# Joint statistics for the two norms around a residual addition, and a first product of four column tiles

## The chip, the cores and the metric

The kernel runs on one NeuronCore of a Trainium2 chip. Its engines are TensorE (PE: matmuls; PEld are its weight loads), VectorE (DVE), ScalarE (ACT), GpSimd (POOL) and SyncE (SP, which here starts the weight DMAs). The metric is the device time of one execution in microseconds, and lower is better. The kernel before takes 2133.98 us (median of three runs, 2133.39 to 2135.55).

## The reference, cut to what matters

The program is a transformer of three blocks over one sequence of 512 positions and 1024 channels. Its first block has a conv layer and an attention layer, and each of them ends in a branch that is normed, gated and added to x, after which x is normed again, scaled and shifted as the input of a gated feed-forward:

```
    for l in range(DEPTH):
        ...
        x = x + g_m * rms_norm(y, norm_g[l, 1])

        h = rms_norm(x, norm_g[l, 2]) * (1.0 + sc_f) + sh_f
        y = conv_ffn(h, ffn_w_in[l], ffn_dw[l], ffn_dwb[l], ffn_w_out[l])
```

Here y is the branch's output (the product with cm_w2 for l = 0, with w_o for l = 1). rms_norm divides each position by the root of its mean square over the 1024 channels. With r the reciprocal root of y's mean square and w = g_m * norm_g[l, 1], the new x is x + w*y*r. The sum of its squares is sum(x²) + 2 r sum(w x y) + r² sum(w² y²): the second norm can be had from three sums that do not need the new x.

## The kernel before, in words

Activations lie transposed: a tile is 128 channels by 512 positions, and there are 8 tiles of x (`XT`), of the normed input h (`Hh`, `Hl`) and of y. Products are done in fp32r with a high and a low part, so a [128 x 128] by [128 x 512] step is three matmuls (`mm3`, lines 291 to 293). Weights come in blocks of 128x1024 from HBM (`fetch`, SP), ACT rounds them to the high part (`split_hi`, line 318) and DVE takes the low part (`split_lo`, line 331). There are three buffers of each part. `split_hi(j)` waits until PE has finished block j-3, `split_lo(j)` follows it, and `fetch(j+3)` waits for `split_lo(j)`.

Each engine's program is written out in order by hand. Generators (`within`, `beside`) interleave side work at each block. In the first feed-forward the side work of DVE is the modulation, a product of 128x1024 (line 629, "mod" below) per step. In the second it is arithmetic on positions (lines 1944 to 1960), which begins with a DMA of the positions that SP starts once the last x tile is written.

A norm goes so: ACT squares the tiles (`square`, line 429), POOL adds six of the eight squares (`gather`, lines 434 and 438), PE sums over the channels with matmuls of a 128x128 slice against a column of ones (`tile_sums`: four matmuls, eight records in the trace, for a tile), DVE makes the mean (`begin_norm`, line 498), POOL the power (`power`, line 518), PE spreads it over the channels (`spread`) into a bank. `fill(n)` issues n matmuls whose result nobody reads.

At the entry of each feed-forward the order is: the norm of y; DVE writes x tile by tile (`add_to_x_dve`, lines 577 and 563), ACT squares it and PE sums (`sums_alone`); a second norm (lines 502, 514, 518, `row_to_cols`); then DVE and ACT make h tile by tile (`make_h_dve`, lines 538 and 543, ACT line 550), while PE multiplies it with the first two column tiles of `ffn_in`. Group by group, two column tiles at a time, each group reads all eight h tiles. After each group ACT takes the two banks (line 1504) and DVE adds two shifted taps (lines 1550 and 1553), which frees the bank; after the second group come the gate and the split of the hidden tile. Five banks rotate: group 0 uses banks 0 and 1, group 1 banks 2 and 3, the next pair of groups 4 and 0, then 1 and 2.

Of the kernel before, what the change touches and what calls it, by code (L numbers as in the profile page):

```python
# [8 lines left out]
F32 = mybir.dt.float32  # L9
# [208 lines left out]
def program(nc, ins, out):  # L218
# [3 lines left out]
    with ctx:  # L222
# [121 lines left out]

        def next_block(hand, name, k0, ahead=AHEAD):
# [77 lines left out]
        ALONE = ("f0", "f1")  # L423
# [17 lines left out]
        def gather_six(s):  # L441
            for t in range(1, 6):
# [10 lines left out]

        def sums_alone(s):
            open_bank(NRM, [(dve_done, ("row", s))])
            fill(11)
            for t in range(DT):
                pe.wait_ge(*act_done["sq", s, t])
                mm(banks[NRM][:, :], ones[:, :], sq[t % 4][:, :], t == 0, t == DT - 1).then_inc(
                    *norm_done.up(("part", s, t), *([("sum", s)] if t == DT - 1 else [])))  # L460
                fill(1 if t < DT - 1 else 3)
# [34 lines left out]
        def begin_norm(s, count, eps=EPS):  # L496
            dve.wait_ge(*norm_done["sum", s])
            dve.e.tensor_scalar(var4, banks[NRM][:, 0:4], 1.0 / count, eps, ALU.mult, ALU.add).then_inc(*dve_done.up(("var", s)))

        def begin_row(s, count):  # L500
            dve.wait_ge(*norm_done["sum", s])
            dve.e.tensor_scalar(part[:, :], banks[NRM][:, :], 1.0 / count, EPS, ALU.mult, ALU.add).then_inc(*dve_done.up(("row", s)))


        def row_to_cols(s):
            open_bank(NRM, [(dve_done, ("var", s))])
            pe.wait_ge(*dve_done["row", s])
            for tb in range(4):
                tok = mm(banks[NRM][:, tb:tb + 1], part[:, tb * P:(tb + 1) * P], ident[:, 0:1], True, True)
            tok.then_inc(*norm_done.up(("cols", s)))  # L510

        def take_cols(s):
            dve.wait_ge(*norm_done["cols", s])
            dve.e.tensor_copy(var4, banks[NRM][:, 0:4]).then_inc(*dve_done.up(("var", s)))
# [80 lines left out]

        def split_ahead(hand):
            presplit(hand, hand.block + AHEAD + 1)
# [2218 lines left out]
```

## Time and profile before

| | us |
|---|---|
| median of 3 runs | 2133.98 |
| the profiled execution | 2137.97 |
| its span in the trace | 2136.2 |
| PE busy in it | 2038.9 (95%) |
| DVE busy | 1294.2 (61%) |
| ACT busy | 853.0 (40%) |
| POOL busy | 169.7 (8%) |

The profiled execution took 3.99 us more than the median, of which 1.8 us lie outside its span. Times in the rows count from the span's start. The first feed-forward's entry runs from about 240 to 318 us, the second's from about 922 to 1005 us.

### The profile page before, as it was taken

The page shows a single profiled execution, that of the slowest core. Times are in us where ns is not written, and L with a number is a line of the kernel's source. Part 1 is how long each engine was busy: PE and PEld are TensorE (multiplying, and loading weights), DVE is VectorE, ACT ScalarE, POOL GpSimd, SP SyncE. Part 2 cuts the span into 40 slices and gives each one's busy share as a digit, 9 for nine tenths or more (in the row PEclk, how much of TensorE's full clock was granted, in tenths as well). Part 3 has the DMA queues.
Part 4 walks back from the last instruction along what each step waited for, and adds up shares of the span by engine and source line. Part 5 has one row for each costly group of instructions (what it writes and reads, how often), then busy time and mean ns, then how long its engine had stood idle before and what let it go on. Part 6 is the DMA issues. An engine that isn't in the chain of part 4 may idle for free.

```text
span 2136.2 us, 26481 instructions
## 1 busy us (share of the span) xinstructions
PE 2038.9 (95%) x10754; PEld 1662.5 (78%) x10756; DVE 1294.2 (61%) x2183; ACT 853.0 (40%) x1430; POOL 169.7 (8%) x112
## 2 busy tenths in 40 slices
PE   5999999999999999899999999999989999999998
PEld 4798778888877976677888887788766788888886
DVE  7666388747836466557765566648876564624632
ACT  3446444324423255534432443332276543412421
POOL 0472100000011000020000000200000010000000
PEclk9999999999999999999999999999999999999999
DMA  8662145655431221112333323222214022332332
GB/s 297 206 209 91 59 148 184 211 195 177 146 110 63 71 68 30 34 46 85 101 107 114 99 93 106 75 78 79 61 49 139 30 90 90 98 99 89 98 99 69
DMA packets 72729, 229.22 MB, mean 107 GB/s; under 512 B 7840, under 2 KB 12832, under 8 KB 72608
## 3 DMA queue, kind: packets, MB, share of 16 engines
q1 hardware_dynamic: 64688, 218.61, 31.7%
q10 hardware_dynamic: 7920, 8.92, 1.2%
q8 instruction: 85, 1.39, 0.3%
q14 instruction: 36, 0.29, 0.0%
HBM read 218.32 MB, written 9.18 MB: 106 GB/s over the span
## 4 chain that ended last, share of the span: by engine, by line
PE 77%; DVE 13%; ACT 5%; issue 3%; POOL 1%; DMA 1%; SPq 0%; DVEq 0%; POOLq 0%; ACTq 0%
PE bank L291 22%; PE bank L293 21%; PE bank L292 21%; PE bank L296 12%; DVE wlo L331 2%; ACT whi L318 1%; PE bank L812 1%; DVE sc L2200 1%; DVE steps L2198 1%; DVE bank L1154 1%; DVE Hl L567 1%; DVE tmp L538 1%; DVE raw L629 1%; DVE Hl L543 1%; DVE XT L563 1%
## 5 line engine op out<-in xcount | busy, mean ns | idle before, releaser
L291 PE MATMUL bank<-Hh,whi 128*128 128x512 f32 x1632 | 653.2, 400 | 22.5 <-DVE wlo L331 9.1
L293 PE MATMUL bank<-Hh,wlo 128*128 128x512 f32 x1632 | 640.7, 393 | 0.0
L292 PE MATMUL bank<-Hl,whi 128*128 128x512 f32 x1632 | 640.5, 392 | 0.0
L331 DVE TENSOR_TENSOR wlo<-stg,whi 128x1024 fp32r<-128x1024 f32 (+1 forms) x299 | 358.5, 1203 | 411.0 <-ACT whi L318 410.5
L318 ACT ACTIVATE whi<-stg 128x1024 fp32r<-128x1024 f32 (+1 forms) x309 | 313.0, 1025 | 395.5 <-PE bank L293 389.2
L291 PEld LDWEIGHTS bank<-Hh,whi 128*128 128x128 f32 x1632 | 309.5, 190 | 94.6 <-DVE wlo L331 12.5
L293 PEld LDWEIGHTS bank<-Hh,wlo 128*128 128x128 f32 x1632 | 309.3, 190 | 65.8
L292 PEld LDWEIGHTS bank<-Hl,whi 128*128 128x128 f32 x1632 | 309.3, 190 | 62.5 <-issue 1.0
L291 PE MATMUL bank<-HIDh,whi 128*128 128x512 f32 x352 | 141.4, 402 | 0.0
L293 PE MATMUL bank<-HIDh,wlo 128*128 128x512 f32 x352 | 137.8, 392 | 0.0
L292 PE MATMUL bank<-HIDl,whi 128*128 128x512 f32 x352 | 137.8, 392 | 0.0
L434 POOL TENSOR_TENSOR part<-sq 128x512 f32<-128x512 f32 x8 | 11.3, 1415 | 1316.3 <-ACT sq L429 1316.3
L291 PE MATMUL bank<-HID2h,whi 128*128 128x512 f32 x256 | 99.7, 389 | 0.0
L293 PE MATMUL bank<-HID2h,wlo 128*128 128x512 f32 x256 | 99.6, 389 | 0.0
L292 PE MATMUL bank<-HID2l,whi 128*128 128x512 f32 x256 | 99.6, 389 | 0.0
L1550 DVE SCALAR_TENSOR_TENSOR tmp<-bank,columns,tmp 128x511 f32<-128x511 f32 x88 | 65.8, 748 | 49.1 <-ACT tmp L1504 49.1
L629 DVE CUSTOM_DVE_ANT_0 raw<-raw,c_act 128x1024 f32<-128x1024 f32 x72 | 87.2, 1219 | 6.6 <-DMA raw<-in_mod_w 6.5
L1504 ACT ACTIVATE tmp<-bank,columns 128x512 f32<-128x512 f32 x88 | 67.8, 770 | 54.7 <-PE bank L293 54.7
L293 PEld LDWEIGHTS bank<-HIDh,wlo 128*128 128x128 f32 x352 | 66.5, 189 | 14.3
L292 PEld LDWEIGHTS bank<-HIDl,whi 128*128 128x128 f32 x352 | 66.5, 189 | 12.7
L291 PEld LDWEIGHTS bank<-HIDh,whi 128*128 128x128 f32 x352 | 66.5, 189 | 12.6
L1513 ACT ACTIVATE HIDh<-tmp 128x512 fp32r<-128x512 f32 x44 | 27.8, 632 | 108.6 <-DVE tmp L1558 108.6
(313 smaller groups left out, 2770.8 us busy)
## 6 DMA issues: line engine op xcount, KB each, us to landing
raw<-in_mod_w SPq DMA_DIRECT2D x96, 512.0 KB, 4.6
stg<-in_ffn_in SPq DMA_DIRECT2D x88, 512.0 KB, 3.9
stg<-in_ff SPq DMA_DIRECT2D x64, 512.0 KB, 3.6
stg<-in_ffn_out SPq DMA_DIRECT2D x40, 512.0 KB, 3.7
stg<-in_cm_w SPq DMA_DIRECT2D x24, 512.0 KB, 4.3
stg<-in_gates SPq DMA_DIRECT2D x16, 512.0 KB, 3.6
stg<-in_z_ch SPq DMA_DIRECT2D x12, 512.0 KB, 3.5
bias_kept<-out_b ACTq DMA_DIRECT2D x20, 256.0 KB, 2.1
```

Of the source, the lines that this page charges most:

```text
L291: pe.e.matmul(out_, l[0], r[0], start=start, stop=False, skip_group_check=True)
L292: pe.e.matmul(out_, l[0], r[1], start=False, stop=False, skip_group_check=True)
L293: return pe.e.matmul(out_, l[1], r[0], start=False, stop=stop, skip_group_check=True)
L296: return pe.e.matmul(out_, l, r, start=start, stop=stop, skip_group_check=True)
L318: act.e.activation(whi[j % NW][:, 0:n * c], stg[j % NSTG][:, 0:n * c], ACT.Copy).then_inc(*w_hi.up(j))
L331: hand.e.tensor_tensor(wlo[j % NW][:, 0:n * c], stg[j % NSTG][:, 0:n * c], whi[j % NW][:, 0:n * c].bitcast(F32), ALU.subtract).then_inc(*m ...
L538: dve.e.scalar_tensor_tensor(tmp[t % 4][:, :], x_tile(t), gain, r[:, :], ALU.mult, ALU.mult).then_inc(*dve_done.up(("hm", ver, t)))
L543: dve.e.scalar_tensor_tensor(Hl[:, t, :], tmp[t % 4][:, :], shift, Hh[:, t, :].bitcast(F32), ALU.add, ALU.subtract).then_inc(*dve_done.up( ...
L629: dve.e.tensor_tensor_reduce(raw[j % NRAW][:, :], raw[j % NRAW][:, :], c_act[:, :], 1.0, 0.0, ALU.mult, ALU.add, modv[:, a:a + 1]).then_in ...
L1504: act.e.activation(at_, bank((("up", l, j), m))[:, :], ACT.Identity, bias=column(bcol + c), scale=column(w3 + 88 + c)).then_inc(*act_done. ...
L1513: act.e.activation(HIDh[:, q, :], at_, ACT.Copy).then_inc(*act_done.up(("hid", l, part, q)))
L1550: dve.e.scalar_tensor_tensor(o[:, 1:S], from_[:, 0:S - 1], column(w3 + 44 + c), o[:, 1:S], ALU.mult, ALU.add).then_inc(*dve_done.up())
```

## The change

The two norms at each feed-forward's entry come from one set of sums. While the branch's last product runs, DVE multiplies y with x and accumulates w·x·y in `tmp[0]` and w²·y² in `tmp[1]` over the first six tiles (conv) or four tiles (attention). PE sums these, and the plain squares, inside the product's last group; the remaining tiles (two or four) are summed each by `joint_tile`, with eight matmuls instead of four. The sum of squares of the old x is kept from the norm before (`keep_var`). A short chain of 128x4 operations on DVE makes the new mean square, POOL raises it, and PE spreads it into bank 5 behind nine fills. Then one loop on DVE makes x and h tile by tile. The first product of the feed-forward works on all four column tiles at once (`gemm_ahead`), the second pair one h tile behind the first. ACT and DVE take its four tiles after all four weight blocks have been passed (`beside_ahead`). The second norm's own squares, sums, row and columns are gone.

The diff, cut to its core:

```diff
         def square(s, t, tile, ready):
             act.wait_ge(*ready)
             if t >= 4:
-                act.wait_ge(*(norm_done["part", s, t - 4] if s in ALONE else pool_done["gathered", s, t - 4]))
+                act.wait_ge(*pool_done["gathered", s, t - 4])
+                if s in GATHERED:
+                    act.wait_ge(*dve_done["acc2", s, t - 4])
...
+        def gather_products(s, Y, g, ready):
+            for t in range(GATHERED[s]):
+                dve.wait_ge(*ready(t))
+                if t > 1:
+                    dve.wait_ge(*dve_done["acc1", s, t - 2])
+                dve.e.tensor_tensor(tmp[2 + t % 2][:, :], Y[t], x_tile(t), ALU.mult).then_inc(*dve_done.up(("xy", s, t)))
+                dve.wait_ge(*act_done["sq", s, t])
...
+                    dve.e.scalar_tensor_tensor(tmp[1][:, :], sq[t % 4][:, :], gain_sq[:, t, 1:2], tmp[1][:, :], ALU.mult,
+                                               ALU.add).then_inc(*dve_done.up(("acc2", s, t)))
...
+                    dve.e.scalar_tensor_tensor(tmp[0][:, :], tmp[2 + t % 2][:, :], g[:, t:t + 1], tmp[0][:, :], ALU.mult,
+                                               ALU.add).then_inc(*dve_done.up(("acc1", s, t)))
+                yield
...
+        def joint_gathered(s):
+            n = GATHERED[s] - 1
+            open_bank(NRM, [(dve_done, ("varx", s))])
+            two_sums(part, pool_done["gathered", s, n], 0, ones[:, 0:1], 1, True, False)
+            two_sums(tmp[1], dve_done["acc2", s, n], 1, ones[:, 0:1], 1, False, False)
+            two_sums(tmp[0], dve_done["acc1", s, n], 8, ones[:, 0:1], 1, False, False)
+
+        def joint_tile(s, t, g):
+            last = t == DT - 1
+            pe.wait_ge(*dve_done["gain_sq", s])
+            two_sums(sq[t % 4], act_done["sq", s, t], 0, gain_sq[:, t, :], 2, False, last)
+            two_sums(tmp[2 + t % 2], dve_done["xy", s, t], 8, g[:, t:t + 1], 1, False, last).then_inc(
+                *norm_done.up(("part", s, t), *([("sum", s)] if last else [])))
+
+        def joint_pe(s, to, g):
+            joint_tile(s, DT - 1, g)
+            fill(3)
+            spread(s, [(dve_done, ("yr", to, DT - 1))])
+            fill(9)
+            spread(to, [(dve_done, ("hm", to, DT - 1))], RX, rx4, pool_done["pow", to])
+            fill(6)
...
+        def joint_dve(s, to, Y, g, gain_, shift_):
+            begin_norm(s, D, at=slice(0, 8, 2))
+            split_ahead(dve)
+            dve.wait_ge(*pool_done["pow", s])
...
+            for t in range(DT):
+                if t > 1:
+                    dve.wait_ge(*dve_done["x", to, t - 2])
+                dve.e.scalar_tensor_tensor(tmp[2 * (t % 2)][:, :], Y[t], g[:, t:t + 1], banks[SPREAD][:, :], ALU.mult,
+                                           ALU.mult).then_inc(*dve_done.up(("yr", to, t)))
+                dve.wait_ge(*dve_done["yr", to, t])
+                dve.e.tensor_tensor(x_tile(t), x_tile(t), tmp[2 * (t % 2)][:, :], ALU.add).then_inc(*dve_done.up(("x", to, t)))
+                if t > 1:
+                    dve.wait_ge(*dve_done["h", to, t - 2])
+                dve.wait_ge(*norm_done["spread", to])
+                dve.wait_ge(*dve_done["x", to, t])
+                dve.e.scalar_tensor_tensor(tmp[2 * (t % 2) + 1][:, :], x_tile(t), gain_[:, t:t + 1], banks[RX][:, :], ALU.mult,
+                                           ALU.mult).then_inc(*dve_done.up(("hm", to, t)))
+                if t == 6:
+                    split_ahead(dve, 1)
+                if t:
+                    low(t - 1)
+            low(DT - 1)
...
+        def gemm_ahead(stage, name, X, by):
...
+            into = [acc_bank((stage, m), by(m)) for m in range(4)]
+            for q in range(DT):
+                product(0, q)
+                if q:
+                    product(1, q - 1)
+            product(1, DT - 1)
+            aside(pe.beside)
+
+        def beside_ahead(hand, name, k0, k1, groups, evac):
+            for _ in range(groups):
+                for i, _ in kparts(k1 - k0):
+                    next_block(hand, name, k0 + i)
+                    aside(hand.beside)
+            for m in range(2 * groups):
+                evac(m)
+            aside(hand.beside)
...
-                    for t in {0: (), 6: (5, 6), 7: (7,)}.get(m, (m - 1,)):
+                    for t in {0: (), 5: (4, 5), 6: (6,), 7: (7,)}.get(m, (m - 1,)):
                         square("cy", t, Y[t], act_done["cy", t])
...
             def tensor():
-                sums_alone(s)
-                row_to_cols(s)
-                fill(4)
-                spread(s, [(dve_done, ("hm", s, DT - 1))])
-                fill(9)
+                gemm_ahead(("up", l, 0), f"ffn_in{l}", HX(s), lambda m: [(dve_done, ("tap2", l, 0, m))])
...
-                beside_gemm(dve, "w_o", 4, DT, 2, evac, 4)
-                gated_gain(gain[1, 1], 1, 2, 1)
-                begin_norm("ay", D)
-                add_to_x_dve("f1", Y, gain[1, 1], [dve_done["gain", 1, 1], norm_done["spread", "ay"]])
+                products = gather_products("ay", Y, gain[1, 1], lambda t: dve_done["ao", t])
+                dve.within[:] = [products]
+                beside_gemm(dve, "w_o", 4, DT, 1)
+                all_of(products)
+                dve.within[:] = []
+                evac_x(4)
+                evac_x(5)
+                beside_gemm(dve, "w_o", 4, DT, 1, evac_x, 6)
+                joint_dve("ay", "f1", Y, gain[1, 1], gain[1, 2], shift(1, 3))
```

How the instructions stand. First PE at the end of the attention layer's last product (tile 6 in bank 0, tile 7 in bank 1; bank 6 takes the sums, `part` the gathered squares, sq2 and sq3 the last two tiles' squares). Before:

```order
L293 MATMUL bank1<-Hh,wlo0 128x512
L296 MATMUL bank6<-ones,part 128x1 x4
L296 MATMUL bank6<-ones,sq2 128x1 x4
L296 MATMUL bank6<-ones,sq3 128x1 x4
L296 MATMUL bank0<-whi1 128x512 x4
L296 MATMUL bank7<-ident,small 128x128 x4
```

After, from the last matmul of tile 7 on:

```order
L293 MATMUL bank1<-Hh,wlo0 128x512
L296 MATMUL bank6<-gain_sq,sq1 128x2 x4
L296 MATMUL bank6<-gains,tmp3 128x1 x4
L296 MATMUL bank6<-gain_sq,sq2 128x2 x4
L296 MATMUL bank6<-gains,tmp2 128x1 x4
L296 MATMUL bank6<-gain_sq,sq3 128x2 x4
L296 MATMUL bank6<-gains,tmp3 128x1 x4
L296 MATMUL bank0<-whi1 128x512 x3
L296 MATMUL bank7<-ident,small 128x128 x4
L296 MATMUL bank0<-whi1 128x512 x9
L296 MATMUL bank5<-ident,small 128x128 x4
L296 MATMUL bank0<-whi1 128x512 x6
```

Ahead of these, inside tile 7, stand 20 more small matmuls: `part`, `tmp1` and `tmp0` between tile 6 and tile 7, and tile 4's eight in the middle of tile 7. The groups of four grew from three to eleven. Second, DVE at the same place: what stands between the low part of the feed-forward's first weight block and the reading of banks 4 and 5 (y's tiles 4 and 5). Before:

```order
L331 TENSOR_TENSOR wlo1<-stg1,whi1 128x1024
L1816 TENSOR_TENSOR Kt<-Kt,bank4 128x512
L1816 TENSOR_TENSOR Kt<-Kt,bank5 128x512
L331 TENSOR_TENSOR wlo2<-stg2,whi2 128x1024
L1816 TENSOR_TENSOR Qt<-Qt,bank0 128x512
```

After:

```order
L524 SCALAR_TENSOR_TENSOR tmp1<-sq2,gain_sq,tmp1 128x512
L531 SCALAR_TENSOR_TENSOR tmp0<-tmp2,gains,tmp0 128x512
L518 TENSOR_TENSOR tmp3<-Kt,XT 128x512
L524 SCALAR_TENSOR_TENSOR tmp1<-sq3,gain_sq,tmp1 128x512
L531 SCALAR_TENSOR_TENSOR tmp0<-tmp3,gains,tmp0 128x512
L1973 TENSOR_TENSOR Kt<-Kt,bank4 128x512
L511 TENSOR_TENSOR tmp2<-Kt,XT 128x512
L1973 TENSOR_TENSOR Kt<-Kt,bank5 128x512
L511 TENSOR_TENSOR tmp3<-Kt,XT 128x512
L331 TENSOR_TENSOR wlo2<-stg2,whi2 128x1024
```

Twelve 128x512 operations, three for each of the tiles 0 to 3, now stand between the split and bank 4; the last five are shown. Third, DVE at the first feed-forward's entry, from the last h tile on. Before:

```order
L543 SCALAR_TENSOR_TENSOR Hl<-tmp3,modv,Hh 128x512
L331 TENSOR_TENSOR wlo2<-stg2,whi2 128x1024
L629 ISA raw0,modv<-raw0,c_act 128x1024
L629 ISA modv 128x1
L331 TENSOR_TENSOR wlo0<-stg0,whi0 128x1024
L1550 SCALAR_TENSOR_TENSOR tmp0<-bank0,columns,tmp0 128x511
L1553 SCALAR_TENSOR_TENSOR tmp0<-bank0,columns,tmp0 128x510
```

After:

```order
L589 SCALAR_TENSOR_TENSOR Hl<-tmp3,modv,Hh 128x512
L732 ISA raw0,modv<-raw0,c_act 128x1024
L732 ISA modv 128x1
L732 ISA raw1,modv<-raw1,c_act 128x1024
L732 ISA modv 128x1
L331 TENSOR_TENSOR wlo1<-stg1,whi1 128x1024
L732 ISA raw2,modv<-raw2,c_act 128x1024
L732 ISA modv 128x1
L331 TENSOR_TENSOR wlo2<-stg2,whi2 128x1024
L732 ISA raw3,modv<-raw3,c_act 128x1024
L732 ISA modv 128x1
L1695 SCALAR_TENSOR_TENSOR tmp0<-bank0,columns,tmp0 128x511
```

Four mods and two splits stand between the last h tile and the taps that free bank 0 (the second of them follows), where one mod and two splits stood. All four tiles' taps follow before the next split.

## Rows read from the trace of the kernel before

**Rows 1.** The page, part 1: busy time and share of the span.

```profile
PE 2038.9 (95%) x10754; PEld 1662.5 (78%) x10756; DVE 1294.2 (61%) x2183; ACT 853.0 (40%) x1430; POOL 169.7 (8%) x112
```

**Rows 2.** Timeline, all engines, conv stage's end: start us, us, engine, line.

```profile
242.27 1.05 PE L296 MATMUL bank<-ones,part 128*128 128x1 f32 x8 [1.67 <-POOL part L438]
...
245.71 1.71 PE L296 MATMUL bank<-ones,sq 128*128 128x1 f32 x8
...
249.73 0.16 DVE L498 TENSOR_SCALAR small<-bank 128x4 f32<-128x4 f32 x1 [10.80 <-PE bank L296]
249.98 1.02 POOL L518 TENSOR_TENSOR small<-small 128x4 f32<-128x4 f32 x1 [7.76 <-DVE small L498]
...
253.44 1.41 DVE L577 SCALAR_TENSOR_TENSOR tmp<-C,gains,bank 128x512 f32<-128x512 f32 x2 [3.54 <-PE bank L296]
...
254.76 0.69 DVE L563 TENSOR_TENSOR XT<-XT,tmp 128x512 f32<-128x512 f32 x1
```

**Rows 3.** Windows: length, busy (x) PE PEld DVE ACT POOL, PEclk, DMA.

```profile
252.00:254.00 2.00, 2.00 (x10) 1.86 (x9) 0.56 (x1) 0.00 (x0) 0.00 (x0) 0.59 0.00 0
...
934.00:936.00 2.00, 2.00 (x17) 1.87 (x16) 0.16 (x1) 0.17 (x1) 0.36 (x1) 1.00 0.07 27
936.00:940.00 4.00, 3.68 (x14) 3.05 (x13) 1.11 (x2) 0.00 (x0) 0.66 (x1) 0.57 0.00 0
```

**Rows 4.** Timeline, DVE and PE, entry of feed-forward 0 and its first column tiles.

```profile
269.11 1.16 PE L296 MATMUL bank<-ident,small 128*128 128x128 f32 x8 [0.32 <-POOL small L518]
...
270.38 1.41 DVE L538 SCALAR_TENSOR_TENSOR tmp<-XT,gains,bank 128x512 f32<-128x512 f32 x2 [2.40 <-PE bank L296]
...
279.85 1.62 DVE L543 SCALAR_TENSOR_TENSOR Hl<-tmp,modv,Hh 128x512 fp32r<-128x512 f32 x2
...
282.81 1.22 DVE L629 CUSTOM_DVE_ANT_0 raw<-raw,c_act 128x1024 f32<-128x1024 f32 x1
...
283.96 1.22 DVE L331 TENSOR_TENSOR wlo<-stg,whi 128x1024 fp32r<-128x1024 f32 x1
...
284.39 0.39 PE L291 MATMUL bank<-Hh,whi 128*128 128x512 f32 x1
...
285.07 0.39 PE L291 MATMUL bank<-Hh,whi 128*128 128x512 f32 x1
...
285.10 0.74 DVE L1550 SCALAR_TENSOR_TENSOR tmp<-bank,columns,tmp 128x511 f32<-128x511 f32 x1
...
287.99 0.75 DVE L1550 SCALAR_TENSOR_TENSOR tmp<-bank,columns,tmp 128x511 f32<-128x511 f32 x1 [1.37 <-ACT tmp L1504]
...
294.60 0.74 DVE L1550 SCALAR_TENSOR_TENSOR tmp<-bank,columns,tmp 128x511 f32<-128x511 f32 x1
...
301.79 1.22 DVE L629 CUSTOM_DVE_ANT_0 raw<-raw,c_act 128x1024 f32<-128x1024 f32 x1
```

**Rows 5.** Timeline, POOL, DVE and PE, attention's end and entry of feed-forward 1.

```profile
923.46 3.53 POOL L438 TENSOR_TENSOR part<-part,sq 128x512 f32<-128x512 f32 x2
...
924.27 1.57 DVE L331 TENSOR_TENSOR wlo<-stg,whi 128x1024 fp32r<-128x1024 f32 x1 [1.65 <-ACT whi L318]
...
932.62 0.95 PE L296 MATMUL bank<-ones,part 128*128 128x1 f32 x8
...
933.43 1.93 PE L296 MATMUL bank<-ones,sq 128*128 128x1 f32 x16
...
935.39 0.16 DVE L498 TENSOR_SCALAR small<-bank 128x4 f32<-128x4 f32 x1 [1.81 <-PE bank L296]
...
955.89 1.41 DVE L538 SCALAR_TENSOR_TENSOR tmp<-XT,gains,bank 128x512 f32<-128x512 f32 x2 [2.47 <-PE bank L296]
...
965.37 1.63 DVE L543 SCALAR_TENSOR_TENSOR Hl<-tmp,modv,Hh 128x512 fp32r<-128x512 f32 x2
...
972.78 0.42 DVE L1944 CAST a<-posi 64x512 f32<-64x512 int32 x1 [4.37 <-DMA posi<-in_pos_q]
...
983.18 0.50 PE L291 MATMUL bank<-Hh,whi 128*128 128x512 f32 x1 [1.49 <-DVE wlo L331]
```

More of the change, by code:

```diff
@@ L343, in presplit, with split_ahead @@
                     fetch(j + NSTG)
+        def split_ahead(hand, more=0):
+            presplit(hand, hand.block + AHEAD + 1 + more)
         def next_block(hand, name, k0, ahead=AHEAD):
@@ L441, in gather_six @@
         def gather_six(s):
-            for t in range(1, 6):
+            for t in range(1, GATHERED.get(s, 6)):
                 gather(s, t)
@@ L494, in fill, with begin_norm @@
                 mm(banks[b][:, :], whi[j % NW][:, 0:P], whi[j % NW][:, 0:S], True, True)
-        def begin_norm(s, count, eps=EPS):
+        def begin_norm(s, count, eps=EPS, at=slice(0, 4)):
             dve.wait_ge(*norm_done["sum", s])
[L498 to L502, printed above, removed]
@@ L505, in row_to_cols @@
[L505 to L514 removed]
+            dve.e.tensor_scalar(var4, banks[NRM][:, at], 1.0 / count, eps, ALU.mult, ALU.add).then_inc(*dve_done.up(("var", s)))
@@ new lines, in weighted, with times_x @@
+        def weighted(s, g):
+            dve.e.memset(gain_sq[:, :, :], 1.0).then_inc(*dve_done.up())
+            dve.wait_ge(*dve_done.now)
+            dve.e.tensor_tensor(gain_sq[:, :, 1], g, g, ALU.mult).then_inc(*dve_done.up(("gain_sq", s)))
+        def times_x(s, t, Y, ready):
+            dve.wait_ge(*ready)
+            if t >= GATHERED[s] + 2:
+                dve.wait_ge(*norm_done["part", s, t - 2])
+            elif t >= GATHERED[s]:
+                dve.wait_ge(*dve_done["acc1", s, GATHERED[s] - 1])
+            dve.e.tensor_tensor(tmp[2 + t % 2][:, :], Y[t], x_tile(t), ALU.mult).then_inc(*dve_done.up(("xy", s, t)))
@@ L516, in power, with joint_act @@
+        def joint_act(to, shift_, used):
+            split_ahead(act)
+            act.wait_ge(*used)
+            for t in range(DT):
+                if t == 5:
+                    split_ahead(act, 1)
+                act.wait_ge(*dve_done["hm", to, t])
+                act.e.activation(Hh[:, t, :], tmp[2 * (t % 2) + 1][:, :], ACT.Identity, bias=shift_[:, t:t + 1]).then_inc(
+                    *act_done.up(("hh", to, t)))
         def power(s):
@@ L701, in gemm_first, with product @@
                             tok.then_inc(*gemm_done.up(*done))
+        def gemm_ahead(stage, name, X, by):
+            blocks = []
+            def product(c, q):
+                while len(blocks) <= 2 * c + q // 4:
+                    blocks.append(next_block(pe, name, 4 * (len(blocks) % 2)))
+                j = blocks[2 * c + q // 4]
+                hi, lo = block_parts(j)
+                xh, xl, ready = X(q)
+                pe.wait_ge(*lo_done(j))
+                pe.wait_ge(*ready)
+                for m in range(2):
+                    o = slice(m * P, (m + 1) * P)
+                    tok = mm3(into[2 * c + m][:, :], (hi[:, q % 4, o], lo[:, q % 4, o]), (xh, xl), q == 0, q == DT - 1)
+                    done = [(stage, 2 * c + m)] if q == DT - 1 else []
+                    if q % 4 == 3 and m == 1:
+                        done.append(("block", j))
+                    if done:
+                        tok.then_inc(*gemm_done.up(*done))
+            into = [acc_bank((stage, m), by(m)) for m in range(4)]
[13 more added lines that the diff above has]
+            aside(hand.beside)
         def beside_first(hand, name):
@@ L1137, in tensor, with gathered @@
                 gemm("w2", "cm_w2", HX("ln"), 0, DT, 1, lambda m: [(act_done, ("cy", m))], 4)
-                pe.within[:] = [sums_within("cy", 6)]
+                def gathered():
+                    for _ in range(6):
+                        yield
+                    joint_gathered("cy")
+                pe.within[:] = [gathered()]
                 gemm("w2", "cm_w2", HX("ln"), 0, DT, 1, lambda m: [(act_done, ("cy", m))], 6)
@@ L1490, in scalar @@
             def scalar():
-                for t in range(DT):
-                    h_high(s, t, shift(l, 3)[:, t:t + 1], [gemm_done[before]])
                 act.beside[:] = [beside_act()]
@@ L1588, in gpsimd @@
             def gpsimd():
-                power(s)
-                pool.wait_ge(*norm_done["sum", s])
                 gather_six(sy)
@@ L1907, in gpsimd @@
                 gather_six("ay")
-                power("ay")
-                pool.wait_ge(*norm_done["sum", "ay"])
+                joint_pool("ay", "f1")
             def sync():
```

116 lines of the change are left out of this document (83 added, 33 removed).

## The prediction

> **What bounds the kernel now.** The page's first part comes first: PE is busy 95% of the span and no other engine over 61% [rows 1]. So the reader looks for stretches in which PE does no useful matmul. The chain of waits names two that the change touches, the entries of the feed-forwards. I then read the timeline of each, and the windows for PE's clock.
>
> At the first entry three marks are enough. V, DVE reads the mean square of y: 249.73 [rows 2]. G, DVE makes the first h product: 270.38 [rows 4]. L, DVE starts the last low part of h: the second of the pair of 1.62, 280.72 [rows 4]. The last h tile is ready at 281.5. PE has 63 matmuls of the first four column tiles left: 15 of group 0 and 48 of group 1. Three take 285.07 - 284.39 = 0.68, one 0.227 [rows 4], so it is through at 295.9 and, with 96 more for the next four tiles (21.8), at E = 317.7. At the second entry V = 935.39, G = 955.89, L = 966.25, and the next four tiles start at 983.18 after a wait of 1.49 for a low part [rows 5], so E = 1005.0. V to G is 20.6 and 20.5: squares, sums and two powers one behind the other. That is what the change attacks.
>
> **What makes V later.** Sums are small matmuls: a group of four (eight records) takes 0.9 at the full clock (24 records from 932.62 to 935.36) and 1.7 at half (245.71) [rows 2, 5]. In the conv stage 3 groups become 7, in attention 3 become 11. The clock decides their price. The doubled price at 245.71 is one sign of it, the windows are the other: 0.59 in 252 to 254; and 0.57 in 936 to 940, though PE was busy 2.00 of 2.00 in 934 to 936 [rows 3], with small matmuls and four fills. So a stretch of sums costs PE its 2.4 GHz and it runs at 1.2.
>
> The Trainium skill ("TensorE: Matmul & The Clock Gate", section "What's actually happening") lets the clock fall after an idle stretch only; a PE that issues sums without a pause would keep 2.4 GHz, and the sum would come out as in the first rival below. The trace disagrees: 0.57 behind a window in which PE was busy 2.00 of 2.00.
>
> Conv: PE now waits 1.67 for the gathered squares and then takes one group [rows 2]. After, the squares come earlier (tile 5 is squared with tile 4), the wait goes and two groups are added (1.8): the last product still ends at 245.8. Then four groups in place of two, at half clock 4 x 1.73 = 6.9: V = 252.7, +3.0.
>
> Attention: DVE's twelve operations for tiles 0 to 3 start behind the split of 924.27, which ends 925.84. POOL is then still adding: two adds take 3.53 beside that split, until 926.99 [rows 5]. I let DVE wait for that end. The Trainium skill ("SBUF — State Buffer", section "Who interferes with whom") calls this an exclusive lock between a DVE operation with two SBUF inputs and a POOL one; without it the sum is 1.2 less. A tensor_tensor takes a step of 0.60 and a scalar_tensor_tensor 0.66 (254.76 - 253.44 for two) [rows 2]; tiles 1 to 3 cost 1.92 each, tile 0 about 1.5 (tensor_scalar on 512 elements from SBUF isn't in the rows; between 0.4 and 0.66, I take 0.47). So w²y² is ready at 933.7. PE reaches the sums when tile 6 is done, 2.72 before 932.6, at 929.9; one group, then idle until 933.7: 2.9 lost. Then, the clock having fallen, two groups (0.9 and 1.75), 6 matmuls (2.6), tile 4's two groups (3.45), 6 matmuls (2.6), and tiles 5, 6, 7 (6 groups, 10.4): V = 955.4, +20.0. At full clock V = 945.4.
>
> **V to G.** Power 1.27 after V (249.98 + 1.02) [rows 2], spread 1.6 at half clock, nine fills of which I let a third run before the clock is back (2.7; 2.0 to 3.9), and 1.27 from the second spread to DVE (269.11 to 270.38) [rows 4]: 6.9. The small chain (five operations of 128x4, each 0.16 as the one at V [rows 2] and a handover, together 1.0) and the second power end at V + 3.5, under the fills. G is 259.6 and 962.3; before, 270.38 and 955.89.
>
> **G to L.** One loop does x and h: yr 0.77 (its follower waits for it), x 0.72, h product 0.66, low part 0.66 = 2.81 for a tile. 0.66 + 7 x 2.81 + the fourth split 1.14 [rows 4] + 0.2 for ACT's last high part = 21.7. Before, 10.34. The loop takes in the 10 us in which x was written before, so here the gain of V to G is given back.
>
> **L to four tiles.** PE takes 12 matmuls (2.72) in each 2.81. The sixth and seventh h tiles come close together behind the split; five products of 6 are left from G + 21.6, so all four tiles are done at G + 28.4. Before, L + 15.2. This is the real saving: 8.5.
>
> **The new wait.** PE's next group needs bank 4 (free) and bank 0, free after tile 0's second tap. In DVE's queue stand before that: mod, mod, split, mod, split, mod. The first split waits for ACT, which waits until PE has finished block 1 at G + 25.9: 27.05. Then split 1.14, mod 1.15, split, mod, taps 0.78 and 0.75 [rows 4]: G + 33.2. PE has come to its fourth matmul at G + 29.1: it waits 4.1. It ends that group at G + 43.4. The next group's first block is split only behind all four tiles' taps: 2.9 for a tile (287.99 - 285.10), again 2.9, then 7.2 (301.79 - 294.60), a mod and the split [rows 4]: G + 47.0, a wait of 3.6. So E = G + 57.9 = 317.5. Queued behind it are only splits and mods of later blocks, which DVE catches up with one group later.
>
> In the second feed-forward arithmetic on positions stands there. Its DMA starts with the last x tile at G + 20.3 and takes 4.0 (an estimate: DVE sat idle 4.37 for it before [rows 5]), the seven casts and products 2.8, then split, step, split, step, taps: bank 0 at G + 32.4, a wait of 3.3. The second wait is 3.2: E = G + 56.7 = 1019.0.
>
> **The sum.** Conv entry 317.5 - 317.7 = -0.2 (V +3.0, V to G -13.7, loop +11.4, tiles -8.5, waits +7.7). Attention entry 1019.0 - 1005.0 = +14.0 (+20.0, -13.6, +11.3, -8.4, and waits 6.5 for 1.7). The gain and square columns at the attention stage's start add four operations of 128x8 on DVE beside a wait for ACT: nothing, at most 0.7; two copies of 128x4 likewise, at most 0.4. Together +13.8: the profiled execution's 2137.97 becomes 2151.8, the median of the runs 2133.98 becomes 2148. Nothing later in either feed-forward gives it back, as PE is dense there.
>
> **The rivals.**
>
> 1. *PE keeps 2.4 GHz through the sums.* Place: behind the last product. Then V = 248.5 and 945.4, V to G is 5.8 (fills 2.0, spread 1.2), E = 312.2 and 1007.9: -5.5 and +2.9, together -2.6: 2131.4, not slower than before. It decides if the clock reads 1.00 from 244 to 254 and from 934 to 950. Against it the 1.71 for a group at 245.71 [rows 2] and the 0.59 and 0.57 of [rows 3]; for it that the 24 records behind 932.62 still ran at full clock [rows 5]. 15%. In part (the clock back in the midst of attention's sums) it gives 2140.
>
> 2. *DVE's backlog does not hold PE.* If bank 0 and the split are there in time, the waits of 7.7 and 6.5 go: 13.8 - 14.2 = -0.4, 2133.6. With half of the waits 2141. With the clock kept too it is 2117, the faster side. For it: DVE is busy only 61% [rows 1]. Against it: its order is fixed, and the 1.49 before 983.18 is such a wait [rows 5]. 12%.
>
> 3. *The thin starts cost the clock as well.* Between G and the third h tile PE is fed six matmuls in 2.8, and each wait of 3 to 4 is idle. If the clock falls at each of these four places as it did in 936 to 940, 4.0 x (1 - 0.57) = 1.7 of work is lost each time [rows 3]: +6.8, 2154.8. For it that 1.67 of idling [rows 2] stands ahead of the slow groups at 245.71. 15%.
>
> **How the numbers follow.** The forecast, with its own spread (fills, POOL, when the clock falls: 2142 to 2152), 58%. A change within 0.2% (2129.7 to 2138.2) can't be told from none here: rival 1 and most of rival 2, 20%. Faster by more: rivals 1 and 2 together or in part, 12%. Slower 68%: forecast, rival 3 and part of the others. The range 2130 to 2156 reaches from rival 1 to rival 3 and leaves out the two together and what is beyond rival 3.
>
> **What would show it.** V near 252 and near 955, with the clock at 0.5 before it; DVE idle about 2 us between its second mod and the next split; PE waits of 3 to 4 on the tap in bank 0 and on a low part in both feed-forwards; PE waiting for `tmp1` near 930 to 934. The forecast is wrong if the clock reads 1.00 in the sums, if V in attention is below 948, or if PE runs without a gap behind its first four tiles.

## The result, and the profile after

The changed kernel takes 2154.48 us (median of 4 runs, 2150.13 to 2157.76), the kernel before 2134.09 us (2133.39 to 2135.55). The ratio is 1.0093, 95% interval 1.0079 to 1.0106: slower by 20 us where 14 were forecast.

The page's first part of the changed kernel, as in [rows 1]: PE's busy time grows by 1.3 us while the span grows by 16.6 (2152.8 for 2136.2). So most of what was added is time in which PE does nothing. The mean granted clock of the span is 0.972, where it was 0.982: within the like busy time more ran slow, which a busy share doesn't show.

```profile
PE 2040.2 (95%) x10762; PEld 1672.1 (78%) x10764; DVE 1322.9 (61%) x2231; ACT 841.5 (39%) x1414; POOL 168.9 (8%) x110
```

The conv stage's end and the first feed-forward's entry, changed kernel, all engines (start us, us, engine, line), to be set beside [rows 2, 4]. V is DVE's reading of y's mean square and G its first h product, as in the prediction. This profile runs 2.72 us ahead of the one before there: ScalarE's evacuation of two of the branch's tiles (L1590, L1435 in the kernel before) starts at 215.48 and not 218.20.

```profile
239.93 1.93 PE L296 MATMUL bank<-ones,tmp 128*128 128x1 f32 x16
243.18 0.95 PE L296 MATMUL bank<-gain_sq,sq 128*128 128x2 f32 x8
246.18 1.03 PE L296 MATMUL bank<-gains,tmp 128*128 128x1 f32 x8
247.25 0.16 DVE L498 TENSOR_SCALAR small<-bank 128x4 f32<-128x4 f32 x1 [1.98 <-PE bank L296]
247.33 1.22 DVE L331 TENSOR_TENSOR wlo<-stg,whi 128x1024 fp32r<-128x1024 f32 x1
247.49 1.93 POOL L624 TENSOR_TENSOR small<-small 128x4 f32<-128x4 f32 x1 [14.33 <-DVE small L498]
251.20 3.65 PE L296 MATMUL bank<-whi 128*128 128x512 f32 x9
254.69 1.05 PE L296 MATMUL bank<-ident,small 128*128 128x128 f32 x8
255.78 0.75 DVE L604 SCALAR_TENSOR_TENSOR tmp<-XT,gains,bank 128x512 f32<-128x512 f32 x1 [2.72 <-PE bank L296]
259.50 0.47 PE L291 MATMUL bank<-Hh,whi 128*128 128x512 f32 x1 [2.37 <-DVE Hl L589]
283.94 1.23 DVE L331 TENSOR_TENSOR wlo<-stg,whi 128x1024 fp32r<-128x1024 f32 x1 [2.99 <-ACT whi L318]
290.09 0.80 PE L291 MATMUL bank<-Hh,whi 128*128 128x512 f32 x1 [3.91 <-DVE tmp L1698]
303.91 0.50 PE L291 MATMUL bank<-Hh,whi 128*128 128x512 f32 x1 [1.00 <-DVE wlo L331]
```

The reader is to see three things. The sums here take 0.95 to 1.05 a group, not 1.7. V is 247.25 and G 255.78, that is 249.97 and 258.50 on the old scale. PE then waits 3.91 for a tap and 1.00 for a low part. The windows of the same stretch (length, busy of PE, PEld, DVE, ACT, POOL, then PEclk) show that the clock falls only behind the sums, and once more in the thin start of the loop. It falls a third time in the wait for the tap (0.55 in 288 to 290).

```profile
246.00:248.00 2.00, 2.00 (x14) 1.74 (x14) 0.75 (x2) 0.16 (x1) 0.51 (x1) 0.81 0.03 8
252.00:254.00 2.00, 2.00 (x6) 1.52 (x6) 1.02 (x2) 0.00 (x0) 0.00 (x0) 0.50 0.00 0
254.00:256.00 2.00, 2.00 (x14) 1.83 (x13) 0.22 (x1) 0.00 (x0) 0.00 (x0) 0.98 0.00 0
262.00:264.00 2.00, 1.76 (x4) 1.49 (x5) 1.93 (x4) 0.28 (x1) 0.00 (x0) 0.50 0.00 0
```

The attention's end and the second feed-forward's entry, changed kernel, beside [rows 5]; this profile is here 0.61 later than the one before (a wait of the last head, at 895.26 and 895.87).

```profile
924.85 1.77 DVE L518 TENSOR_TENSOR tmp<-Kt,XT 128x512 f32<-128x512 f32 x1
928.99 0.95 PE L296 MATMUL bank<-ones,part 128*128 128x1 f32 x8
932.59 2.94 PE L296 MATMUL bank<-ones,tmp 128*128 128x1 f32 x16 [2.65 <-DVE tmp L524]
938.09 1.70 PE L296 MATMUL bank<-gain_sq,sq 128*128 128x2 f32 x8
952.45 1.85 PE L296 MATMUL bank<-gains,tmp 128*128 128x1 f32 x8
954.34 0.16 DVE L498 TENSOR_SCALAR small<-bank 128x4 f32<-128x4 f32 x1 [6.07 <-PE bank L296]
962.63 0.75 DVE L604 SCALAR_TENSOR_TENSOR tmp<-XT,gains,bank 128x512 f32<-128x512 f32 x1 [2.49 <-PE bank L296]
996.22 0.50 PE L291 MATMUL bank<-Hh,whi 128*128 128x512 f32 x1 [3.29 <-DVE tmp L1698]
1009.74 0.50 PE L291 MATMUL bank<-Hh,whi 128*128 128x512 f32 x1 [3.02 <-DVE wlo L331]
```

PE waits 2.65 for DVE's gathered products. The two groups behind that wait take 2.94 together, and from then every group of sums costs 1.70 to 1.85. The windows from 934 to 958 all read 0.50.

### The profile page after: what moved, and what is told of

The parts are those of the page before. It is cut to its first block, busy times and chain, and to the rows that moved or that the text cites. A ratio compares the mean times of both kernels' runs of the same rounds, so it can differ in the third digit from the quotient of the medians.

```text
span 2152.8 us, 26519 instructions
## 1 busy us (share of the span) xinstructions
PE 2040.2 (95%) x10762; PEld 1672.1 (78%) x10764; DVE 1322.9 (61%) x2231; ACT 841.5 (39%) x1414; POOL 168.9 (8%) x110
## 4 chain that ended last, share of the span: by engine, by line
PE 78%; DVE 13%; ACT 5%; issue 3%; POOL 1%; DMA 0%; SPq 0%; DVEq 0%; POOLq 0%; ACTq 0%
PE bank L291 22%; PE bank L293 21%; PE bank L292 21%; PE bank L296 12%; DVE wlo L331 2%; ACT whi L318 1%; PE bank L952 1%; DVE sc L2365 1%; DVE steps L2363 1%; DVE bank L1298 1%; DVE Hl L673 1%; DVE XT L669 1%; ACT pr L927 1%; DVE tmp L683 1%; POOL small L624 0%
## 5 line engine op out<-in xcount | busy, mean ns | idle before, releaser
L443 POOL TENSOR_TENSOR part<-sq 128x512 f32<-128x512 f32 x8 | 11.3, 1417 | 1346.5 <-ACT sq L438 1346.5
```

## The experiments

Ratios are to the kernel before, run on the same chip; "the changed kernel" is 1.0093. To place a difference I use two stretches of each trace: *conv*, from a wait of 0.91 that all kernels have ahead of the branch's last products (L1070 in the kernel before, at 195.93) to the first matmul on HIDh, the hidden tiles of the feed-forward; and *attention*, from the wait of the last head named above to the wait at 1287.77 of the profile before (1303.50 in the changed one).

### The conv entry alone

The attention's entry is taken back to the kernel before; the same holds for the second feed-forward:

```diff
-        GATHERED = {"cy": 6, "ay": 4}
+        GATHERED = {"cy": 6}
+        ALONE = ("f1",)
...
-                joint_tile("ay", 6, gain[1, 1])
-                joint_pe("ay", "f1", gain[1, 1])
+                sum_last("ay")
+                fill(4)
+                spread("ay", [(dve_done, ("yr", "f1", DT - 1))])
```

> The conv stage's entry as changed, the attention's entry and the second feed-forward's start as before. By the prediction's terms (conv entry -0.2 us, attention entry +14.0 us) this kernel takes as long as the one before: 2134 to 2136 us. Read from the two traces (from the first product of cm_w2 to the sums of the next norm 417.1 us before, 418.3 after) it is +1.2: 2135.3 us. The rival, that the cost of a joint norm is alike at both entries (both have the half clock and the wait for the first tile's tap), gives half of the 20 us: 2144 us.

Measured: 2139.93 us, 1.0029 (1.0019 to 1.0040). So 0.64% or 13.7 us of the loss belong to the attention, as forecast (14.0), and 6.2 us come from somewhere else, where -0.2 stood. But the trace of the conv stretch doesn't show them: 210.08 us, and 210.34 in the changed kernel; the kernel before has 208.82 in its first profile and 210.07 in the second (below). Neither theory was right: the 6.2 lie outside the stretch, and where they come from is taken up below.

### Two products of two tiles

```diff
-                gemm_ahead(("up", l, 0), f"ffn_in{l}", HX(s), lambda m: [(dve_done, ("tap2", l, 0, m))])
...
-                    for j in range(max(a // 2, 1), b // 2):
+                    for j in range(a // 2, b // 2):
...
```

> Both joint norms kept, but each feed-forward's first four column tiles as two products of two tiles, one after the other, instead of one loop of four. If the loop of four is worth what the prediction gave it (8.5 us per entry, since h comes only every 2.83 us and a product of two tiles needs 1.36 us of it), less the waits for the first taps that the loop of four brings (3.9 and 3.3 us), this takes 4 to 8 us more per entry: 2162 to 2171 us, the value 2166 us. The rival, that the waits behind the loop give back all that it gains, has 2154 us, within 2 us of the changed kernel.

Measured: 2158.08 us, 1.0120 (1.0106 to 1.0133), 0.27% above the changed kernel: 3 us for each entry, the intervals just touching. PE's waits between 255 and 400 in that kernel (what for: us, times, longest):

```profile
PE bank L291 <- DVE Hl L589: 11.4, 7, 2.9
```

The loop of four has 3.4 us of waits for h there and 4.9 for a tap and a split, with half clock around each, so 8.3 against 11.4. I had asked the wrong sum: the 8.5 of the prediction stood beside 7.7 of new waits, so 0.8 was to be expected in the conv stage, not 4 to 8. From V to the end of the stretch it is 156.5 against 154.7 in the conv stage and 352.0 against 349.2 in the attention, so the loop of four is worth some 2 to 3 us an entry. The whole stretches differ by less (210.48 against 210.34, 409.56 against 407.63), as V came 1.6 and 1.0 us earlier in this one profile.

### The first taps earlier

```diff
...
+            for i in steps[:-1]:
+                next_block(hand, name, k0 + i)
+            evac(0)
+            next_block(hand, name, k0 + steps[-1])
+            for m in range(1, 2 * groups):
+                evac(m)
+            for _ in range(len(steps) + 1):
+                aside(hand.beside)
```

> As the changed kernel, but in the feed-forwards' first loop VectorE and ScalarE evacuate the first column tile before the split of the last of the four weight blocks, and the modulation (or rotation) work that stood between the splits comes behind all four evacuations. In the changed kernel's trace PE waits 3.9 us and 3.3 us for the first tile's second tap, and then 1.0 and 3.0 us for a low part of weights. If these waits come from the order on VectorE, 5 us go of the 11: 2149 us (2147 to 2152). The rival is that VectorE's backlog is conserved, so the PE waits for a later split or tap instead: 2154 us, within 1.5 us of the changed kernel.

Measured: 2162.78 us, 1.0137 (1.0123 to 1.0151): 9 us slower than the changed kernel. The wait for the tap went to 0.5 us, and the next group's low part came late. The timeline, DVE and PE, of this kernel:

```profile
299.01 0.69 DVE L1708 TENSOR_TENSOR HIDl<-tmp,HIDh 128x512 fp32r<-128x512 f32 x1 [0.70 <-ACT HIDh L1664]
304.60 1.23 DVE L732 CUSTOM_DVE_ANT_0 raw<-raw,c_act 128x1024 f32<-128x1024 f32 x1 [0.33 <-DMA raw<-in_mod_w]
306.94 1.23 DVE L331 TENSOR_TENSOR wlo<-stg,whi 128x1024 fp32r<-128x1024 f32 x1 [1.10 <-ACT whi L318]
308.22 0.80 PE L291 MATMUL bank<-Hh,whi 128*128 128x512 f32 x1 [10.92 <-DVE wlo L331]
```

Five modulations, 6.2 us, stand between the last tap's tile and the split. So on this order the split must stay ahead of them.

### The modulations later, the splits where they are

```diff
-                    aside(hand.beside)
+                    if not later:
+                        aside(hand.beside)
...
+            if later:
+                owed[hand] = [5, 0]
...
```

`later` holds in the first feed-forward alone, for DVE and for SP's loads.

> As the changed kernel, but in the first feed-forward's first loop the five modulation columns of VectorE (and their loads on SyncE) are put off, one each to every second later group; the splits of weights stay where they are. Two of them, 1.1 us each, stand before the first tap at 288.5 us, for which PE waits 3.9 us. If VectorE's order there is the cause, the wait falls by 2.2 us and the next by up to 1: 2152 us. The rival, that later taps and splits take over the wait, has 2154.5 us within 1 us. The kernel that evacuated the first tile earlier had one wait of 10.9 us for a split in place of the two, so a result above 2156 us would say that the splits are what counts.

Measured: 2152.20 us, 1.0094 (1.0081 to 1.0107), where the changed kernel has 1.0093: no change, the rival. Waits of PE between 284 and 420, first this kernel, then the changed one:

```profile
PE bank L291 <- DVE wlo L331: 4.7, 6, 2.5
PE bank L291 <- DVE tmp L1711: 1.6, 1, 1.6
```

```profile
PE bank L291 <- DVE tmp L1698: 3.9, 1, 3.9
PE bank L291 <- DVE wlo L331: 1.0, 1, 1.0
```

2.3 us go from the tap and 3.7 come back at six splits. DVE's work stays the same and only its place moves; DVE is 61% busy over the kernel, but 80 of 96 us between 304 and 400.

### The attention's sums behind the product

```diff
-                    yield
-                    joint_gathered("ay")
-                    yield
-                    joint_tile("ay", 4, gain[1, 1])
-                    yield
-                    joint_tile("ay", 5, gain[1, 1])
+                    for _ in range(6):
+                        yield
+                    joint_gathered("ay")
+                    joint_tile("ay", 4, gain[1, 1])
+                    joint_tile("ay", 5, gain[1, 1])
```

> As the changed kernel, but at the attention's entry the three sums of the gathered tiles and those of tiles 4 and 5 stand behind the last product of w_o instead of within it. If sums within the product cost it its clock (12 of its matmuls take 0.63 us at 0.50 instead of 0.39, with 0.43 instead of 0.23 us from start to start: 2.4 us) and hold it for VectorE's gathered products (2.65 us, of which some 1.5 go), this kernel takes 3 to 4 us less: 2151 us. The rival: the clock falls in any case, and the last product x with y on VectorE now waits for tile 4's sums, so the chain only moves: 2154 to 2157 us.

Measured: 2151.07 us, 1.0079 (1.0065 to 1.0093): 3.4 us less by the medians and 3.0 by the ratios, as expected, but the intervals overlap. In its trace no wait for `tmp` is left, and V comes 53.2 us behind the last head's wait, not 58.5. That second number is soft. The other five traces whose attention sums stand as in the changed kernel have V 54.5 to 58.7 us behind it, as a different number of their groups ran at half clock: in the one with 54.5 (the short chain, below) six of the eleven ran at full clock in between, 1.03 us or less each.

### Wide matmuls between the sums

This starts from the kernel just told.

```diff
+                for _ in range(n):
+                    mm(banks[2][:, :], Hh[:, DT - 1, 0:P], Hh[:, DT - 1, :], True, True)
```

> As the kernel with the attention's sums behind the product (2151.1 us), with one more matmul of 512 columns, whose result is never read, after each of the groups of four small matmuls but the last (10 in all). If wide matmuls between the small ones hold TensorE's clock at 1.00, each of the eleven groups takes 0.95 instead of 1.85 us (9.9 us less) and the wide ones cost 10 times 0.23: 2143.5 us. If the clock stays at 0.50 whatever stands between, the wide ones cost 10 times 0.43: 2155.4 us.

Measured: 2150.35 us, 1.0085 (1.0072 to 1.0098), against 1.0079 without them: no difference that the intervals show. So of the two expected numbers neither came. In the traces the stretch from the first sum to V is 18.5 us with them and 15.9 without. Windows of this kernel:

```profile
930.00:934.00 4.00, 4.00 (x35) 3.88 (x34) 3.84 (x6) 1.42 (x3) 0.00 (x0) 1.00 0.00 0
934.00:936.00 2.00, 2.00 (x13) 1.86 (x12) 1.18 (x2) 0.79 (x1) 0.00 (x0) 0.70 0.01 4
936.00:944.00 8.00, 8.00 (x37) 7.71 (x36) 2.62 (x5) 2.21 (x3) 0.00 (x0) 0.50 0.21 68
```

The clock falls from 1.00 to 0.50 with PE busy throughout (14.00 of 14.00), and the wide matmuls did not hold it: without them it fell at the same place (0.97 in 934 to 936, 0.50 behind), after four groups at full clock in both. Both numbers of the expectation assumed one clock for all eleven groups, and there are two. PE waits for nothing between 925 and 950 in either kernel.

### Three quarters of two tiles' sums left out

```diff
+            n = 1 if s == "ay" and t in (4, 5) else 4
-            two_sums(sq[t % 4], act_done["sq", s, t], 0, gain_sq[:, t, :], 2, False, last)
+            two_sums(sq[t % 4], act_done["sq", s, t], 0, gain_sq[:, t, :], 2, False, last, n)
```

> As the changed kernel, but of the attention's tiles 4 and 5 only the first of four row blocks is summed, so 12 of their 16 small sums are left out (both norms there are wrong by this part). In the changed kernel's trace the four groups take 1.70, 1.85, 1.70 and 1.85 us at half clock; if PE is what sets the end of this stretch, three quarters of that go: 5.3 us, 2149.2 us. The rival: VectorE's products or ScalarE's squares of tiles 6 and 7 end last there, so only 1 us or less goes: 2153.5 us or more.

Measured: 2148.54 us, 1.0071 (1.0058 to 1.0084): 5.9 us less than the changed kernel by the medians, 4.7 by the ratios. That fits the 5.3 that the rows give for 12 small matmuls on PE's path and speaks against the rival's 1 us, though the intervals overlap by a little (1.0079 to 1.0084). In its trace V comes 6.1 us earlier, but there the clock was back for the last four groups (three at 1.03 us, one at 1.53), so its parts can't be set against the rows.

### A short chain between the two powers

```diff
             begin_norm(s, D, at=slice(0, 8, 2))
-            split_ahead(dve)
             dve.wait_ge(*pool_done["pow", s])
...
+            split_ahead(dve)
...
-            fill(9)
+            fill(4)
```

> As the changed kernel, but VectorE's split of weights comes behind the six small instructions that derive the second mean square and not before them (the first power on GpSimd took 1.93 us beside that split, 1.01 us without), and the fill between the two spreads is 4 wide matmuls instead of 9 (3.65 us at half clock for the nine). If the second spread waited for the fill, G comes 2.2 to 2.9 us earlier per entry and the time is 2149.5 us. The rival: the fill is what brings TensorE's clock back to 1.00 (it read 0.50 before it and 0.99 in 254:256), so the first loop starts at half clock and gives the gain back: 2154 to 2157 us.

Measured: 2147.61 us, 1.0068 (1.0056 to 1.0080): 0.25% or 5.3 us less. POOL and DVE of this kernel at the attention's end:

```profile
948.90 0.16 DVE L498 TENSOR_SCALAR small<-bank 128x4 f32<-128x4 f32 x1 [4.25 <-PE bank L296]
949.14 1.02 POOL L624 TENSOR_TENSOR small<-small 128x4 f32<-128x4 f32 x1 [23.02 <-DVE small L498]
951.23 1.91 POOL L567 TENSOR_TENSOR small<-small 128x4 f32<-128x4 f32 x1 [1.07 <-DVE small L584]
954.39 0.75 DVE L604 SCALAR_TENSOR_TENSOR tmp<-XT,gains,bank 128x512 f32<-128x512 f32 x1 [0.59 <-PE bank L296]
```

V to G is 5.5 in both stages (8.5 and 8.3 in the changed kernel), 5.8 us less in all. The two edits were made together, so their shares are not shown. The slow power moved with the split: it is 1.02 where the split isn't and 1.91 where it is, now the second of the two, and DVE starts the h product 1.25 us after its end. The Trainium skill ("SBUF — State Buffer", section "Who interferes with whom") has this as an exclusive lock between a DVE operation with two SBUF inputs and POOL; the two rows agree.

### The kernel before, with 64 bytes more

What is left is the 6.2 us that no wait shows. The feed-forwards' second products (down products, on the hidden tiles HIDh, and HID2h in the third feed-forward) have no idle time and clock 1.00, yet they were longer. `gain_sq` is a new tile of 64 bytes per partition, and all tiles allocated later stand 64 bytes further on. So the kernel before gets a tile of that size which nothing uses:

```diff
         ROT = sb("ROT", [P, S])
+        sb("spare", [P, 2 * DT])
```

> The kernel before with nothing changed but 64 bytes per partition, never read or written, allocated where the changed kernel allocates gain_sq, so that every tile allocated later stands 64 bytes further. In the changed kernel's trace the down products, which are never idle and at clock 1.00, take 65.94 and 51.65 us where they took 65.28 and 51.14 us, and the matmuls that read HIDh have a mean of 395 ns where it was 389 to 390 in 304:630. If the place of those tiles is the cause, this kernel is 2 to 3 us slower than before: 2135.7 us. The rival, that the place is nothing and it is the new order of the work, has 2133 us, no change.

Measured: 2142.22 us, 1.0033 (1.0020 to 1.0047): 4 to 10 us slower, with no instruction added or moved. But its eight executions fall into two groups: three at 2133.53 to 2136.06 us with a mean granted clock of 0.984 or 0.985, and five at 2142.06 to 2144.15 with 0.980. The kernel before has such executions too: 17 at 0.984 or 0.985 with a mean of 2132.3 us, and two at 0.980, of 2138.1. At like clocks the shift costs 2.7 and 4.8 us; the rest of the 7.0 is that more of these executions lost clock, and why they did isn't shown.

The profile is of the first group. The groups of the third feed-forward's down product (xcount | busy us, mean ns), first the kernel before in its second profile, then this one:

```profile
L291 PE MATMUL bank<-HID2h,whi 128*128 128x512 f32 x256 | 99.7, 389 | 0.0
L293 PE MATMUL bank<-HID2h,wlo 128*128 128x512 f32 x256 | 99.6, 389 | 0.0
L292 PE MATMUL bank<-HID2l,whi 128*128 128x512 f32 x256 | 99.6, 389 | 0.0
```

```profile
L292 PE MATMUL bank<-HID2h,whi 128*128 128x512 f32 x256 | 101.1, 395 | 0.0
L294 PE MATMUL bank<-HID2h,wlo 128*128 128x512 f32 x256 | 100.4, 392 | 0.0
L293 PE MATMUL bank<-HID2l,whi 128*128 128x512 f32 x256 | 99.5, 389 | 0.0
```

The changed kernel has the same 395, 392 and 389. Its first down product (96 groups of three matmuls) takes 65.94 us from start to start of what follows, this kernel's 65.94, that of the kernel before 65.28: 6.9 ns a group. It is 65.28 in all four traces without the 64 bytes and at least 65.94 in all ten with them. 352 such groups on HIDh and 256 on HID2h make 4.2 us, an estimate for those two tiles alone.

### The changed kernel without the shift

```diff
-        gain_sq = sb("gain_sq", [P, DT, 2])
+        gain_sq = cols(2 * DT).rearrange("p (t c) -> p t c", c=2)
```

> The changed kernel with gain_sq in 16 free columns of the tile small, so that all later tiles stand where they stood before. If the place of the tiles costs 2 to 3 us, this is 2150.4 us and the down products take 65.28 and 51.14 us again; if not, 2153 us, as the changed kernel.

Measured: 2152.09 us, 1.0085 (1.0073 to 1.0097). The down product is 65.28 again:

```profile
L291 PE MATMUL bank<-HID2h,whi 128*128 128x512 f32 x256 | 99.8, 390 | 0.0
L293 PE MATMUL bank<-HID2h,wlo 128*128 128x512 f32 x256 | 99.7, 390 | 0.0
```

By the medians 2.4 us go and by the ratios 1.7. That is near the 2 to 3 that I had expected and less than the 4.2 of the rows; the intervals of the two kernels overlap so far that they allow 4.2 and nothing alike. The rows say which term it is; the times give it 1.7 here and 7.0 with the kernel before (2.7 to 4.8 at like clocks), and the 4.2 of the rows lies between. Of the 6.2 us of the conv entry alone it leaves 2.0, which no run places.

### The kernel before, profiled again

> The kernel before, profiled once more. Its first profiled execution took 2137.97 us, 4 to 5 more than the median of its runs, and its granted clock fell to 0.50 and 0.72 in 104:112, where the other traces mostly read 1.00. If that fall is a matter of the single execution, this one takes 2133 to 2135 us and has the clock at 1.00 there; if it belongs to the kernel, it takes 2138 us again.

Measured: 2133.94 us, span 2132.1. The window in question, in the first profile and in this one:

```profile
104.00:108.00 4.00, 4.00 (x18) 3.81 (x17) 3.82 (x6) 2.12 (x4) 4.00 (x2) 0.50 0.89 303
```

```profile
104.00:108.00 4.00, 4.00 (x21) 3.41 (x21) 3.86 (x6) 2.10 (x4) 4.00 (x3) 1.00 0.93 280
```

As expected, it was a matter of the execution. Of the same kernel, the first profile has 208.82 and 392.51 us in the two stretches and the second 210.07 and 389.98: the clock falls in other places each time. A difference of 1 to 3 us between two single profiles proves nothing here, nor does one of 4 us in the attention's sums.

### The best of it

The conv entry alone, with the short chain and without the shift; the attention as before.

> The change at the conv stage's entry alone, with the split of weights behind the small chain, four fills for nine, and gain_sq in free columns of small. From the kernel with the conv entry alone (1.0029 of before, 2139.3 us) the chain takes half of what it took at both entries (2.7 us) and the place of the tiles 2.5 us: 2134 us, about the kernel before. The rivals: the place is worth nothing, 2136.6 us; or the conv entry's cost lies in the joint norm itself and both edits miss it, 2139 us.

Measured: 2129.76 us, 0.9980 (0.9972 to 0.9989): faster than the kernel before by 2.3 to 6.0 us. The conv stretch is 207.14 us; it is 210.07 both in the second profile of before and in the changed kernel without the shift. The 2.9 are the V to G of 5.5, where the latter has 8.2. What the ratio gives beyond that, 1.4 us, isn't explained, nor why it came out 4 us below the 2134 expected.

## Why the prediction was right, and where it was not

The forecast of 2148 was 6.5 us low, within its range, and the side was right. The changed kernel came out at the number of rival 3 (2154.8), but by other terms, as the list below shows. The steps are compared with the shifted kernel before, which shares the changed one's places of tiles.

| stretch | predicted | measured |
|---|---|---|
| conv: V | +3.0 | +0.7 |
| conv: V to G | -13.7 | -11.9 |
| conv: G to the end | +10.6 | +11.8 |
| attention: V | +20.0 | +19.9 |
| attention: V to G | -13.6 | -11.3 |
| attention: G to the end | +7.7 | +8.7 |
| place of the tiles (from rows, see above) | not in the sum | +4.2 |

- **Conv entry -0.2.** Right as a sum: 0.5 (against the shifted kernel) and 0.0 (without the shift, second profile of before). But that is luck in part: V came 2.3 us earlier than forecast and the rest 3.0 us longer. V was earlier since rival 1 came true here: the clock held from 239 to V, at 247.25, which the prediction itself had named as a sign of being wrong. It does not always hold: in the short chain's trace, with these sums in the same order, it fell at 239 and V came 2.9 us later than here. V to G was 8.5 and not 6.9: the nine fills took 3.65 for 2.7, and the first power 1.93, beside the split, for 1.02. That was a lock I had used for the attention's POOL and overlooked here.
- **Attention entry +14.0.** Right in mechanism, 2 to 3 us small by the traces: 16.2 (unshifted pair) and 17.3 (shifted pair), but 13.7 by the ratios. PE waited 2.65 for `tmp` (2.9 predicted) and of the eleven groups nine ran at half clock. That V agrees to 0.1 us is luck, as other traces of the same sums have it up to 4 us earlier. One cause in it was wrong: I let DVE wait for POOL's adds; DVE started at 924.85 beside them, and its first product took 1.77 where the next took 0.68. The cost is nearly the 1.2 that I had given it.
- **The new waits.** First 3.91 and 3.29 (4.1 and 3.3 predicted), second 1.00 and 3.02 (3.6 and 3.2). The DVE pause before the split was 2.99, about 2 predicted. The conv stage's second wait is short as PE itself was slow at 0.50 before it.
- **Rival 3.** Its mechanism is there: 0.50 in 262 to 264 and in 968 to 974, and 0.50 in 290 to 294 behind the first wait for a tap; behind the second, the clock stayed at 1.00. From G to the end of the four tiles is 29.5 and 29.4 where 28.4 was predicted, and from G to the end of the next four 59.1 and 58.1 where 57.9 and 56.7 were. So it cost 1.2 to 1.4 us an entry net of the shorter waits, not 3.4. I had it as an alternative and it belongs in the sum.
- **Rival 2** fell: moving the backlog moved the wait (two experiments).
- **The step that failed** is the sum itself: "Nothing later in either feed-forward gives it back" speaks of waits, and the sum put at nothing, without a word, that a new tile moves all later ones. The unshifted pair's 0.0 and 16.2 with 4.2 for the place make 20.4; the ratio gives 19.9 (16.9 to 22.6).
- **The clock in sums.** The prediction set the row (0.57 behind a window of 2.00 of 2.00) against the Trainium skill ("TensorE: Matmul & The Clock Gate", section "What's actually happening"), by which the clock falls behind an idle stretch. The wide-matmul experiment bears the row out without any pause: 0.50 behind 6.00 of 6.00. What exactly tips it stays open: in the changed kernel's profile the conv stage's seven groups all ran at full clock and nine of the attention's eleven at half, while in the short chain's profile four of the seven ran at half and the clock came back for six of the eleven.

## What to carry to other kernels

Fold two norms into one only if their sums can be gathered off TensorE: each group of four small matmuls on its path costs 0.9 us, and 1.8 once the clock has fallen, and the attention has eight groups more than before. Look at what stands between two short steps of a chain before touching the steps: a split moved and five fills fewer were together worth 2.7 us an entry. When a small tile is added, put it where no large one moves, and time the kernel before with the same shift. And before two profiles are compared, look at the granted clock in each: in this kernel it moved a single step by up to 4 us.

## What was not expected of the hardware

- 64 bytes more ahead of a moving operand made its matmuls 6 ns (389 to 395) and 3 ns (389 to 392) longer with the same clock; the low half, which is shifted too, stayed at 389. Why the two halves differ isn't settled, nor which offsets are good.
- The clock falls in other places in each execution of one kernel: it read 0.50 and 1.00 in 104 to 108, with PE busy 4.00 of 4.00 in both.
- The clock fell to 0.50 in a run of small matmuls although PE was busy for 6 us without a pause (930 to 936) and a wide matmul stood behind each group.
